# Moving the fourth modulation product's row sums, the last one's early chunks and some PSUM copies in a hybrid attention, short-convolution and expert-choice MoE step

## The reference, cut to what matters

```python
m = jax.nn.silu(cond) @ w_ada + b_ada            # 2 conditions, 2048 x 12288
sh1, sc1, g1, sh2, sc2, g2 = split(m, 6)
h = rms_norm(x, g_norm1) * (1 + sc1) + sh1
q, k, v, bg, cg, u = split(h @ w_in)
attn = block_attention(...)                       # 8 heads, 2 kv heads
conv_out = bg * short_conv(cg * u, conv_w)        # depthwise, width 3
mixed = concat([rms_norm(attn), rms_norm(conv_out)])
x = x + g1 * (mixed @ w_out)
h2 = rms_norm(x, g_norm2) * (1 + sc2) + sh2
x = x + g2 * ec_moe(h2, w_router, w_gate, w_up, w_down)   # 16 experts
```

## Time and profile before

| | |
|---|---|
| median of 3 runs | 1519.86 us (1519.55 to 1520.50) |
| the profiled execution, its own time | 1520.56 us |
| its span | 1518.9 us |
| PE, DVE, ACT, POOL busy | 95%, 41%, 17%, 2% |
| HBM read, written | 565.02 MB, 6.55 MB |
| q, k, v and the modulations before it | to 188 us |
| conv steps 0 to 23 | about 178 to 446 us |
| output projection | 446 to 588 us |
| router to first expert matmul | 588 to 601 us |
| experts and the end | 601 to 1519 us |

### The profile page before, as it was taken

One profiled execution on the slowest core, in us unless ns is written; L12 is line 12 of the kernel. 1 busy time (PEld: TensorE's weight loads), 2 busy tenths in 40 slices (PEclk: granted clock), 3 DMA queues, 4 the chain that ended last, 5 costly groups with the idle time before them and its releaser, 6 DMA issues.

```text
span 1518.9 us, 18489 instructions
## 1 busy us (share of the span) xinstructions
PE 1448.1 (95%) x7806; PEld 882.3 (58%) x7806; DVE 623.8 (41%) x1033; ACT 255.1 (17%) x358; POOL 26.7 (2%) x58
## 2 busy tenths in 40 slices
PE   6999999999999999999999999999999999899998
PEld 3667799888899997435434335335335335335433
DVE  5454977877799996101301301301301301211313
ACT  4233223333234223000000000000000000000200
POOL 0000000000000000000000000000000000000000
PEclk9999999999999999999999999999999999999999
DMA  9999697777778759999999999999999999999999
GB/s 374 403 395 367 251 332 291 280 259 262 260 274 294 256 172 382 389 433 431 433 431 429 431 433 431 431 432 433 431 431 432 433 430 430 432 433 429 430 423 352
DMA packets 99856, 572.48 MB, mean 377 GB/s; under 512 B 9613, under 2 KB 54613, under 8 KB 76757
## 3 DMA queue, kind: packets, MB, share of 16 engines
q1 hardware_dynamic: 88416, 520.14, 84.0%
q0 software_dynamic: 6912, 50.33, 8.7%
q10 hardware_dynamic: 4468, 1.14, 0.3%
HBM read 565.02 MB, written 6.55 MB: 376 GB/s over the span
## 4 chain that ended last, share of the span: by engine, by line
PE 69%; DMA 23%; DVE 4%; SPq 2%; issue 2%; ACT 1%; DVEq 0%; ACTq 0%
PE psum L653 67%; DMA ring<-in_w_up 18%; DMA ring<-in_w_ada 3%; SPq L563 2%; DMA res<-in_w_ada 1%; DVE res L1664 1%; DMA ring<-in_w_down 1%; DVE w_parts L1537 1%; PE psum L663 0%; DVE ring L1685 0%; PE psum L852 0%; PE psum L1104 0%; SPq L450 0%; PE psum L1074 0%; ACT w_parts L1237 0%
## 5 line engine op out<-in xcount | busy, mean ns | idle before, releaser
L653 PE MATMUL psum<-ring,hid 128*64 128x512 f32 x3024 | 685.6, 601 | 46.4 <-DMA ring<-in_w_up 32.9
L653 PEld LDWEIGHTS psum<-ring,hid 128*64 128x64 f32 x3024 | 243.6, 139 | 464.9 <-issue 416.0
L2000 DVE TENSOR_TENSOR hid<-psum,hid 128x512 f32<-128x512 f32 x16 | 11.1, 692 | 515.0 <-PE psum L653 515.0
L653 PE MATMUL psum<-h_parts,w_parts 128*128 128x384 f32 x1152 | 207.3, 337 | 1.0 <-DVE hid L1713 1.0
L653 PEld LDWEIGHTS psum<-h_parts,w_parts 128*128 128x128 f32 x1152 | 199.8, 188 | 4.8 <-issue 2.5
L1537 DVE TENSOR_TENSOR w_parts<-ring,w_parts 128x2048 fp32r<-128x2048 f32 x52 | 119.0, 2288 | 47.6 <-ACT w_parts L1237 47.3
L1237 ACT ACTIVATE w_parts<-ring 128x2048 fp32r<-128x2048 f32 x52 | 99.6, 1916 | 194.9 <-PE psum L653 163.0
L653 PE MATMUL psum<-w_parts,h_parts 128*128 128x512 f32 x432 | 103.3, 395 | 0.6 <-DVE h_parts L1581 0.6
L653 PE MATMUL psum<-ring,early 128*32 128x512 f32 (+6 forms) x654 | 92.9, 539 | 7.8 <-DMA ring<-in_w_ada 6.7
L653 PEld LDWEIGHTS psum<-w_parts,h_parts 128*128 128x128 f32 x432 | 79.7, 188 | 25.5 <-issue 9.2
L653 PEld LDWEIGHTS psum<-early,mix 128*128 128x128 f32 x768 | 86.6, 192 | 9.0 <-issue 9.0
(11 more groups left out here) (223 smaller groups left out, 725.7 us busy)
## 6 DMA issues: line engine op xcount, KB each, us to landing
ring<-in_w_up SPq DMA_DIRECT2D x30, 4096.0 KB, 22.7
ring<-in_w_gate SPq DMA_DIRECT2D x28, 4096.0 KB, 29.3
ring<-in_w_down SPq DMA_DIRECT2D x26, 4096.0 KB, 28.7
ring<-in_w_ada POOLq DMA_DIRECT2D x48, 1024.0 KB, 6.8
ring<-in_w_in SPq DMA_DIRECT2D x36, 1024.0 KB, 8.2
ring<-in_w_ada SPq DMA_DIRECT2D x28, 768.0 KB, 15.5
res<-in_w_ada SPq DMA_DIRECT2D x16, 1024.0 KB, 7.2
ring<-in_w_out SPq DMA_DIRECT2D x16, 1024.0 KB, 5.8
```

Source lines behind the costliest of these rows:

```text
L653: return nc.tensor.matmul(out, lhsT, rhs, start=start, stop=stop, skip_group_check=True)
L2000: tt(by_row, bank[1][:, :].rearrange("p (b a) -> p a b", a=4), by_row, ALU.mult).then_inc(act_ready, 1)
```

## The change

1. `chunk_add` and `chunk_load` work in column halves: each half of `chunk_3` has a semaphore of its own, SP reloads a half when that half is added; 4 DVE instructions and 2 loads a chunk in place of 2 and 1.
2. The 16 chunks of modulation 3 are added at the end of conv steps 1 to 16 (before: 1 to 4, 6, 8 to 11, 13 to 19). The sum over partitions, its copy and its transpose come one step earlier, and so does the move of modulation 4 (`perm_move(4)`).
3. Modulation 5 is added in three conv steps, 20, 21 and 22 (chunks 1, 2, 3), where before it was 21 and 22 (chunks 1, 2). Output step 6 loses its two adds. The place of the PE event for its chunk 0 stays.
4. `router()` runs at output step 6, not 10.
5. ACT copies the u columns (`conv_copy`, 8 copies of 128x384) and the 12 attention outputs from PSUM; DVE did both.

```diff
-CONV_ADDS = [1, 2, 3, 4, 6, 8, 9, 10, 11, 13, 14, 15, 16, 17, 18, 19]
-CONV_SUMS = 20
+CONV_ADDS = list(range(1, KC + 1))
+CONV_SUMS = 19
-EARLY_ADDS = {21: 2, 22: 2}
-EARLY = 4
+EARLY_ADDS = {20: 2, 21: 2, 22: 2}
+EARLY = 6
-ADDS_AT = {s: 2 for s in (2, 4, 5, 6, 7, 8, 9, 10, 11, 12, 13)} | {3: 1, 14: 3}
+ADDS_AT = {s: 2 for s in (2, 4, 5, 7, 8, 9, 10, 11, 12, 13)} | {3: 1, 14: 3}
...
             def chunk_load(k):
-                if k:
-                    sp.wait_ge(add_done_3, 2 * k)
-                else:
-                    sp.wait_ge(x_saved, 16 * X_PARTS)
-                sp.dma_start(chunk_3, ada_rows[k * P:(k + 1) * P, 3 * D:4 * D]).then_inc(chunk_in, 16)
+                for half in range(2):
+                    if k:
+                        sp.wait_ge(add_done_3, 4 * (k - 1) + 2 * half + 2)
+                    else:
+                        sp.wait_ge(x_saved, 16 * X_PARTS)
+                    cols = slice(half * D // 2, (half + 1) * D // 2)
+                    sp.dma_start(chunk_3[:, cols], ada_rows[k * P:(k + 1) * P, 3 * D:4 * D][:, cols]).then_inc(chunk_in[half], 16)
...
-                if s - 4 == 19:
+                if s - 4 == 18:
                     perm_move(4)
...
+            def conv_copy(b, j):
+                if j == 0:
+                    if b:
+                        a.wait_ge(conv_out, 2 * b)
+                    a.wait_ge(conv_acc, b + 1)
+                else:
+                    a.wait_ge(unit_used, U_QKV + 2 * b + 2)
+                copy(cu[:, j, :], bank[1 + j][:, 0:T]).then_inc(conv_out, 1)
+
             for s in range(U_CONV + 1):
                 hi_part(U_QKV + s + 1)
+                if s % 6 == 2:
+                    conv_copy(s // 2 - 1, 1)
...
                 n = s - ATT - 6
                 if 0 <= n < ATT_UNITS:
+                    a.wait_ge(o_done, n + 1)
+                    if n < CTX_UNITS:
+                        copy(mixT[:, 2 * n:2 * n + 2, 0:P], bank[7][:, 0:2 * P].rearrange("p (h t) -> p h t", h=2)).then_inc(o_out, 1)
+                    else:
+                        copy(mixT[:, n - CTX_UNITS, P:T], bank[7][:, 0:2 * P]).then_inc(o_out, 1)
...
+                if s % 6 == 1:
+                    conv_copy(s // 2, 0)
...
             def chunk_add(k):
-                v.wait_ge(chunk_in, 16 * (k + 1))
...
+                for half in range(2):
+                    cols = slice(half * D // 2, (half + 1) * D // 2)
+                    v.wait_ge(chunk_in[half], 16 * (k + 1))
+                    for n in range(2):
+                        sums, rows = added_up_3[n][:, cols], chunk_3[:, cols]
...
-                if s == 10:
+                if s == 6:
                     router()
```

More of the change, by code:

```diff
@@ L348, in build @@
         ones_set, add_done = sem("ones_set"), sem("add_done")
-        x_saved, x_back, chunk_in, add_done_3, summed_3 = sem("x_saved"), sem("x_back"), sem("chunk_in"), sem("add_done_3"), sem("summed_3")
+        x_saved, x_back, add_done_3, summed_3 = sem("x_saved"), sem("x_back"), sem("add_done_3"), sem("summed_3")
+        chunk_in = [sem("chunk_in0"), sem("chunk_in1")]
         moe_landed = [sem(f"moe_landed{n}") for n in range(WIDE)]
@@ L892, in _ @@
                     pe.wait_ge(ones_set, 3)
-                    pe.wait_ge(add_done_3, 2 * KC)
+                    pe.wait_ge(add_done_3, 4 * KC)
                     pe.wait_ge(o_out, ATT_UNITS)
@@ L1655, in chunk_add @@
             def chunk_add(k):
-                v.wait_ge(chunk_in, 16 * (k + 1))
                 if k == 0:
                     v.wait_ge(x_saved, 16 * X_PARTS)
[L1659 to L1664, removed]
+                for half in range(2):
[3 more added lines that the diff above has]
+                        sums, rows = added_up_3[n][:, cols], chunk_3[:, cols]
+                        if k == 0:
+                            ts(sums, rows, cond[:, k, n:n + 1], None, ALU.mult).then_inc(add_done_3, 1)
+                        else:
+                            v.wait_ge(add_done_3, 4 * (k - 1) + 2 * half + n + 1)
+                            stt(sums, rows, cond[:, k, n:n + 1], sums, ALU.mult, ALU.add).then_inc(add_done_3, 1)
             adds = [0]
@@ L1705, in conv_chunk @@
             def conv_chunk(b, j):
+                if b % 3 == 0:
+                    return
                 src = bank[1 + j][:, 0:T]
@@ L1711, in conv_chunk @@
                     v.wait_ge(unit_used, U_QKV + 2 * b + 2)
-                if b % 3 == 0:
-                    copy(cu[:, j, :], src).then_inc(conv_out, 1)
-                elif b % 3 == 1:
+                if b % 3 == 1:
                     v.wait_ge(conv_out, 2 * b + j - 1)
@@ L1780, in _ @@
                 if 0 <= n < ATT_UNITS:
[L1781 to L1785, removed]
                     v.wait_ge(osq_ready, n + 1)
```

## The result

The changed kernel takes 1528.18 us (median of 6 runs, 1526.96 to 1528.96), the kernel before beside it 1520.06 (1519.55 to 1520.50): the ratio is 1.0053, with a 95% interval of 1.0044 to 1.0063. The difference of the medians is 8.1 us, where 7.84 was forecast. The profiled execution of the changed kernel took 1527.5 us, its span is 1525.7.

A forecast was written before the change was run, and what follows sets the result against it. PE bounds the kernel up to the experts, where the DMA engines are full, so a delay of PE's arrival there moves the end. +8.7 - 0.86 = +7.84 us gives a median of 1527.7 us, range 1524.2 to 1531.2.

The forecast's parts named there:

- The stop (the part that costs): Conv step 22: DVE waits for chunk 2's load, so L1716 starts 9.7 us late and PE stands 6.8 us.
- What is caught up (1.0 us): From conv step 22 to the conv norm: DVE can regain only 1.0 us of its 9.7 us delay.
- The forecast of 8.7: At the conv norm: DVE, and PE behind it, come 8.7 us late, 9.7 less 1.0.
- Output projection (-0.86): PE's wait at 552.42 goes, as the router takes the place of two adds in output step 6: -0.86 us.
- the 0.16 us of the earlier trace: PE's wait at 466.88, behind the conv norm's chain of DVE and ACT, left unchanged by the forecast.
- The wait of step 20 (-1.03): PE's wait at 412.93 for the u columns' copy goes, by ACT's copies and missing adds: -1.03 us, inside the 8.7.
- The sum: Whole kernel: +8.7 - 0.86 = +7.84 us, 1527.7 us on the median.
- The tight place, step 6: Adds at step 5 delay the j = 1 bank to 244.7; PE needs it at 245.3: fits by 0.6 us, taken as 0.
- The clock: PE after the stop runs partly at 1.2 GHz, losing 1.5 us; free in step 22 or 23 through 2.5 us spare.
- No stop at all: Rival: PE's step 22 does not hang on chunk 2, only the gains are left: 1518.0 us; 7%.
- The experts give back 2 to 4 us: Rival, expert stage: the ring could be fuller when PE arrives and the stream catch up: 1524 to 1526 us; 8%.
- More than one stop: Rival: step 6 stalls by 1, the clock adds 1.5, or chunk 2 takes 8.4 to land: 1529 to 1531; 20%.

The follow-up runs named there:

- two kernels with the stop undone: Changed kernel with two early chunks of modulation 5 in place of three: added at steps 21 and 22, 1520.13 us; at steps 20 and 22, 1519.62 us.
- the 14 matmuls: 14 identity matmuls ahead of the last router matmuls: in the kernel before, 1522.77 us; in the changed kernel with early adds at 20 and 22 only, 1522.06 us.

## Why the prediction was right, point by point

- **The stop (the part that costs).** Right in place and cause, and 0.6 us too long. PE's event at 426.95 (forecast 427.06), POOL's issue at 428.35 (428.45), DVE's adds from 433.44 (433.95), L1741 at 437.97 (438.55), PE's wait 6.17 us (6.8). The load took 5.1 us, where I took 5.5 between 5.0 and 8.4: with the copy of x and the small moves out of the way it was nearly the shortest. The event moved to step 20 shows that the wait, not the work, is the price.
- **What is caught up (1.0 us).** DVE came 9.12 us late to L1741 and the squares' sum 7.95 late (458.15 against 450.20), so 1.17 was caught up. The forecast of 8.7 up to there was 0.75 too high, mostly for the load.
- **Output projection (-0.86).** The first expert matmul is 6.77 us late, so 1.18 came back, not 0.86. The wait of 0.86 went with the router's move, as the router's return shows, and 1.16 of the 1.18 came back at that place: the term is right in kind and was sized by the idle time that the row shows, which is 0.3 less than what the wait costs. I had left the 0.16 us of the earlier trace rows untouched, and it went too, but ahead of the matmul at 474.83, so it lies within the 7.95.
- **The wait of step 20 (-1.03).** This is the weakest step, though it hardly moves the sum. I took a wait of one execution as a cost of every run, and two of three executions do not have it; where it stood it cost 1.31, not 1.03. It may be why two kernels with the stop undone measure 1520.13 and 1519.62, and not the 1518.6 that their first expert matmul (1.4 us early) promised; that is not shown, as the intervals end close to that value. I put the gain down to ACT's copies and the moved adds together. Each alone sufficed in its one trace: with ACT's copies PE did not wait although the chunk add was late, and with the adds at steps 1 to 16 no chunk add stands ahead of the copy.
- **The sum, and some luck.** The terms as the traces show them give 7.95 - 1.18 = 6.77 us, 1.1 less than the 7.84 forecast. The medians differ by 8.1: the profiled execution of before was 0.5 us over its median and that of the changed kernel 0.7 under it. The first may be the wait of step 20; the second has no cause on record. That the median came within 0.5 us of 1527.7 is luck in part.
- **The tight place, step 6.** DVE took the bank out from 243.93 to 244.5 (forecast 244.1 to 244.7), PE did not wait, and four halves took 4.87 us (4.7 to 4.9):

```profile
239.14 4.87 DVE L1689 SCALAR_TENSOR_TENSOR res<-res,early 128x1024 f32<-128x1024 f32 x4
243.93 0.55 DVE L1744 TENSOR_TENSOR mix<-psum,hid 128x384 f32<-128x384 f32 x1
```

- **The clock.** A stop of 6.2 us did bring the lower level, and the lost work was 15.05 - 12.76 = 2.3 us where I had taken 1.5; the 2.1 us that PE waits for DVE when the clock is kept, where I had counted 2.5, were just enough. The warning of the Trainium skill ("TensorE: Matmul & The Clock Gate", section "Why this matters for your kernels"), that gaps between bursts of matmuls put the array back at half rate, agrees with the windows above (0.66 behind the stop). The lower rate did not lengthen the run here, where DVE sets the pace up to the norm.
- **The rivals.** No stop at all: refuted by the row of 6.17 us. The experts give back 2 to 4 us: the 14 matmuls arrive at the end with 2.84 and 2.91 of their 3.2 us, and the changed kernel's expert stage is as long as before (917.6 and 917.5 us). More than one stop: step 6 did not stall, the clock cost nothing that the medians show, and the load came early.

## What to carry to other kernels

Before work is moved to an earlier step, ask of each of its inputs what lets its load be issued, and not only when the engine would have time for it: a load into a buffer that is freed by a later step of another engine can't be early, and all that is queued behind the waiting instruction pays. Here one index in a list of places, the step of the event that frees the buffer, was worth 7.5 us. And a small wait in one trace is not yet a cost of the kernel: look for it in a second execution before its removal is put into a sum, and size it by the start times on either side, and not by the idle time that the line shows.

## What the hardware showed that I had not expected

- A stop of 6.2 us of PE was followed by the lower clock in two thirds of the next 7.5 us; with identity matmuls in the stop, in two kernels, the clock stayed at the full level and the 72 matmuls took 12.76 us in place of 15.05. Two more executions with a stop had 14.67 (after 7.52 us) and 14.07 (after 6.18), so the loss is not the same each time.
- Short waits of PE cost 0.3 us more than the idle time shown: 1.03 cost 1.31 (step 20 of before), 0.86 cost 1.16 (output step 12).
- A float32 matmul of 128x128 on the identity counts twice in the trace (86 records for 43, 54 for 27) and takes 0.22 to 0.23 us in all.
- The 1 MB load of chunk 2 took 5.1 us when little else was in flight, and about 6.0 before, with the copy of x beside it (6.0 is worked out from the mean of two, 7.2, and the second's 8.4; that the copy of x is the cause is not shown).
